# A one-core three-block network: norm roots, pair sums and final squares put in another order

## The reference, cut to what matters

```python
def rms_norm(x, g):                     # before every part
    return x * rsqrt(mean(x * x, -1) + 1e-6) * g
def sq_relu_mlp(h, w_up, w_down):       # 1024 -> 4096 -> 1024, twice
    return square(relu(h @ w_up)) @ w_down
# layer 0: x += rglru_mixer(norm(x)); x += sq_relu_mlp(norm(x), ...)
# layer 1: x += dsa_mixer(norm(x));   x += sq_relu_mlp(norm(x), ...)
# x = rms_norm(x, final_norm_g)
# second network: h = rmsnorm(x); q, k, v, r, lr, u, g_a, g_b = split(h @ w_in)
#   linear attention over chunks of 64 with decays from lr; gates; x += merged @ w_out
#   gate, up = split(rmsnorm(x) @ w_ffn_in); x += (silu(gate) * up) @ w_ffn_out   # 2816 wide
# out = rmsnorm(x, norm_final)
```

## Time and profile before

| | us |
|---|---|
| median of 3 runs (lowest to highest) | 1854.32 (1854.08 to 1855.75) |
| profiled execution | 1855.39 |
| its span, first to last instruction | 1854.1 |
| TensorE busy | 1809.6 |
| VectorE, ScalarE, GpSimd busy | 1301.1, 797.7, 282.8 |
| mean granted TensorE clock | 0.989 |

### The profile page before, as it was taken

The page is one execution under the profiler, slowest core; times in us unless marked ns, Lnnn a source line. Parts: engine busy times, 40 slices in busy tenths (PEclk is TensorE's granted clock), DMA queues, the critical chain, the costliest instruction groups (busy, mean ns, idle before and its releaser), DMA issues.

```text
span 1854.1 us, 21884 instructions
## 1 busy us (share of the span) xinstructions
PE 1809.6 (98%) x8584; PEld 1463.9 (79%) x8584; DVE 1301.1 (70%) x1694; ACT 797.7 (43%) x1046; POOL 282.8 (15%) x227
## 2 busy tenths in 40 slices
PE   9999899999999999899999989999999999999998
PEld 7788688888877668688888868788787888788886
DVE  7885878686879865677786857766446446856757
ACT  6743434343444863334343344555323333323324
POOL 0004000000145864000000051111001321001010
PEclk9999899999999999999999989999999999999999
DMA  6233150522233103341405022221332324331411
GB/s 229 91 114 113 46 161 30 173 91 91 64 97 121 40 4 111 113 140 43 159 25 180 21 80 81 79 68 60 95 97 89 104 69 159 100 127 47 148 57 57
DMA packets 146374, 174.98 MB, mean 94 GB/s; under 512 B 7296, under 2 KB 120064, under 8 KB 146272
## 3 DMA queue, kind: packets, MB, share of 16 engines
q1 hardware_dynamic: 144256, 166.45, 27.6%
q0 software_dynamic: 2016, 7.14, 1.1%
HBM read 171.31 MB, written 2.14 MB: 94 GB/s over the span
## 4 chain that ended last, share of the span: by engine, by line
PE 85%; DVE 5%; issue 4%; ACT 3%; POOL 2%; DMA 0%; SPq 0%; DVEq 0%; POOLq 0%; ACTq 0%
PE bank L968 26%; PE bank L970 26%; PE bank L969 26%; PE bank L1004 1%; PE bank L1183 1%; DVE wlo L1995 1%; PE bank L1209 1%; ACT whi L1447 1%; DVE XC L2092 1%; PE bank L1320 1%; PE bank L1338 1%; POOL Hw L952 1%; DVE rstd L2011 1%; PE bank L1187 1%; POOL wlo L772 0%
## 5 line engine op out<-in xcount | busy, mean ns | idle before, releaser
L968 PE MATMUL bank<-Ahi,whi 128*128 128x512 f32 x1400 | 552.0, 394 | 12.4 <-DVE wlo L1995 5.8
L970 PE MATMUL bank<-Ahi,wlo 128*128 128x512 f32 x1400 | 546.1, 390 | 0.0
L969 PE MATMUL bank<-Alo,whi 128*128 128x512 f32 x1400 | 546.0, 390 | 0.0
L1995 DVE TENSOR_TENSOR wlo<-stage,whi 128x2048 fp32r<-128x2048 f32 (+1 forms) x133 | 306.4, 2304 | 158.6 <-ACT whi L1447 158.5
L1447 ACT ACTIVATE whi<-stage 128x2048 fp32r<-128x2048 f32 (+1 forms) x139 | 262.6, 1889 | 228.5 <-PE bank L970 203.1
L968 PEld LDWEIGHTS bank<-Ahi,whi 128*128 128x128 f32 x1400 | 262.9, 188 | 78.2 <-DVE wlo L1995 8.0
L970 PEld LDWEIGHTS bank<-Ahi,wlo 128*128 128x128 f32 x1400 | 262.8, 188 | 56.3
L969 PEld LDWEIGHTS bank<-Alo,whi 128*128 128x128 f32 x1400 | 263.0, 188 | 55.3 <-issue 1.2
L968 PE MATMUL bank<-whi,Hh 128*128 128x512 f32 x602 | 238.2, 396 | 15.9 <-issue 13.8
L969 PE MATMUL bank<-wlo,Hh 128*128 128x512 f32 x602 | 236.5, 393 | 0.0
L970 PE MATMUL bank<-whi,Hl 128*128 128x512 f32 x602 | 236.4, 393 | 0.0
(11 more groups left out here) (358 smaller groups left out, 2467.3 us busy)
## 6 DMA issues: line engine op xcount, KB each, us to landing
stage<-in_mlp_w_up SPq DMA_DIRECT2D x32, 1024.0 KB, 5.4
stage<-in_w_in SPq DMA_DIRECT2D x22, 1024.0 KB, 5.1
stage<-in_w_ffn_in SPq DMA_DIRECT2D x22, 1024.0 KB, 4.9
quad<-in_mlp_w_down SPq DMA_DIRECT2D x16, 1024.0 KB, 6.1
stage<-in_mlp_w_down SPq DMA_DIRECT2D x16, 1024.0 KB, 4.9
stage<-in_rec_w_in SPq DMA_DIRECT2D x6, 1024.0 KB, 5.3
stage<-in_att_w_in SPq DMA_DIRECT2D x6, 1024.0 KB, 5.3
stage<-in_rec_w_out SPq DMA_DIRECT2D x4, 1024.0 KB, 5.7
```

The source lines that it names most:

```text
L968: e.matmul(ps, hi, rh, start=first, stop=False, skip_group_check=onto)
L969: e.matmul(ps, hi, rl, start=False, stop=False, skip_group_check=onto)
L970: return e.matmul(ps, lo, rh, start=False, stop=last, skip_group_check=onto)
L1995: e.tensor_tensor(lo_of(u)[:, 0:nk, 0:n], source(u), f32(hi_of(u)[:, 0:nk, 0:n]), ALU.subtract).then_inc(s_lo[slot_of[u]], 1)
```

## The change

- MLP and feed-forward part: the root matmul stands after block 0, not after block 1.
- MLP, on VectorE and ScalarE: `first_of_pair` of a pair stands behind the relu of its second tile, `second_of_pair` behind the relu of the next tile, `low_sums` a pair later; `high_sums` behind the next square; weights' low halves ahead of the relu.
- The differences: in group 0 (`early(key)` false) T3 is formed inside the slab, after the sums of product 1, and after T2; T1 is formed a step later. In other groups T1 and T3 stay ahead of the slab. In the feed-forward part `first_of_pair` stands ahead of the difference.
- The high half of the second unit after an MLP (qi0, Q0) is made inside the last slab.
- Linear attention: ScalarE makes all eight Ahi and then the sixteen squares, then K0's and V0's high halves; VectorE makes the low halves of Q0, K0 and V0 one behind the other. The two norm matmuls stand after qk1 and use banks 6 and 7 outside the ring.
- The end: partial squares of half rows in a tile of their own (ysum), the gain multiplied in by GpSimd, rows 0 and 1 and the right halves of rows 2 and 3 scaled by ScalarE.

```diff
-            if m == 1:
+            if m == 0:
...
     pair(("Q", 0), ("qk", 2))
-    ring.add("ss", "ss2")
     pair(("K", 0), ("qk", 1), ("qk", 3))
...
+    DIFF = [{"T1": 1, "T2": 2, "T3": 3, "T4": 4}, {"T1": 1, "T3": 2, "T2": 3, "T4": 4}]
+
+    LAST = [(0, 0), (1, 0), (0, 1), (1, 1), (2, 1), (3, 1), (2, 0), (3, 0)][:6]
+
+    def early(key):
+
+        return key[-1] > 0
...
+        e.wait_ge(s_cols, 32)
+        for i, (j, h) in enumerate(LAST):
+            e.wait_ge(s_ysq, i + 1)
+            e.tensor_tensor(sum_of(j, h), sum_of(j, h), fin2b[:, h * 512:h * 512 + 512], ALU.mult).then_inc(s_yw, 1)
...
         product(("qk", 2), s, 128, Ahi, Alo)
-        ps = begin("ss")
-        e.wait_ge(s_tsp, 14)
-        e.matmul(ps[:, :], ones[:, :], sqa_e[:, :], start=True, stop=True).then_inc(*ring.put("ss"))
-        ps = begin("ss2")
-        e.matmul(ps[:, :], ones[:, :], sqb_e[:, :], start=True, stop=True).then_inc(*ring.put("ss2"))
         s = take_unit(("K", 0))
         product(("qk", 1), s, 0, Ahi, Alo)
+        e.wait_ge(s_tsp, 14)
+        e.matmul(banks[6][:, :], ones[:, :], sqa_e[:, :], start=True, stop=True).then_inc(s_ss, 1)
+        e.matmul(banks[7][:, :], ones[:, :], sqb_e[:, :], start=True, stop=True).then_inc(s_ss, 1)
         product(("qk", 3), s, 128, Ahi, Alo)
...
                     turn_x(1, 0, 1)
+                    root("root_f", "ffn")
                 product(("fg", g, j + 1), s, 128, Ahi, Alo)
                 if g == 0 and j == 0:
                     turn_x(1, 2, 3)
-                    root("root_f", "ffn")
...
                         squared(l, 8 * g + 2 * mm - 1)
                     for u in w[mm]:
                         hi(u)
+                    if mm == 0 and g == 0:
+                        std_of(("root", l), 1024)
+                    squared(l, 8 * g + 2 * mm)
                     if mm:
                         high_sums(n0 + mm - 1)
-                    elif g == 0:
-                        std_of(("root", l), 1024)
-                    squared(l, 8 * g + 2 * mm)
                 squared(l, 8 * g + 7)
                 after = u_of[(*key, "T4")] + 1
-                slab_hi(key, [after, after + 1] if g < 3 else [after])
+                slab_hi(key, [after, after + 1])
...
             scaled_hi(m, gfm[:, m:m + 1])
-            if n == 7:
-                hi(u_of["lr"] + 1)
-            for i, (acc, t, kw) in enumerate(((sqa_e, sqt_e, {}), (sqb_e, sqs_e, {"scale": c1("fin1", m)}))):
-                if n > 2:
-                    e.wait_ge(s_tsp, 2 * (n - 3) + i + 1)
-                e.activation((t[n % 2] if n else acc)[:, :], X[:, m, :], ACT.Square, **kw).then_inc(s_tsa, 1)
+            if n < 7:
+                return
+            for n, m in enumerate(TURN):
+                for i, (acc, t, kw) in enumerate(((sqa_e, sqt_e, {}), (sqb_e, sqs_e, {"scale": c1("fin1", m)}))):
+                    if n > 2:
+                        e.wait_ge(s_tsp, 2 * (n - 3) + i + 1)
+                    e.activation((t[n % 2] if n else acc)[:, :], X[:, m, :], ACT.Square, **kw).then_inc(s_tsa, 1)
...
-        hi(u_of["Q", 0] + 1)
-        e.wait_ge(*ring.full("ss"))
-        e.activation(std[:, :], ring.bank("ss")[:, :], ACT.Sqrt, bias=epsc[:, 0:1], scale=1.0 / 1024).then_inc(s_std, 1)
-        e.wait_ge(*ring.free("ss2"))
+        hi(u_of["K", 0])
+        hi(u_of["V", 0])
+        e.wait_ge(s_ss, 1)
+        e.activation(std[:, :], banks[6][:, :], ACT.Sqrt, bias=epsc[:, 0:1], scale=1.0 / 1024).then_inc(s_std, 1)
+        e.wait_ge(s_ssr, 2)
         e.activation(sqt2[:, :], sqb_e[:, :], ACT.Sqrt).then_inc(s_std, 1)
-        hi(u_of["K", 0] + 1)
-        hi(u_of["K", 0] + 2)
+        hi(u_of["V", 1])
...
+        last_square(0, 0, 0, 1)
+        last_square(1, 1, 0, 1)
+        last_square(2, 0, 1, 4)
+        last_square(3, 1, 1, 4)
+        e.wait_ge(s_ysq, 4)
         for j in range(2):
-            e.wait_ge(*product_read(key, 4, j))
-            e.wait_ge(*product_read(key, 1, j))
-            if j:
-                e.wait_ge(s_ysq, j)
-            e.activation(junk[:, :], D[j][:, :], ACT.Square, accum_out=oss[:, j:j + 1]).then_inc(s_ysq, 1)
-        e.wait_ge(s_ysq, 2)
-        e.activation(rtok[:, 0:2], oss[:, 0:2], ACT.Sqrt, bias=epsc[:, 0:1], scale=1.0 / 1024).then_inc(s_yroot, 1)
+            last_root(j)
+        last_square(4, 2, 1, 5)
+        last_square(5, 3, 1, 5)
         for j in range(2):
-            e.wait_ge(*product_read(key, 5, j))
-            e.wait_ge(s_ysq, 2 + j)
-            e.activation(junk[:, 0:512], sum_of(2 + j, 1), ACT.Square, accum_out=oss[:, 4 + j:5 + j]).then_inc(s_ysq, 1)
-        for j in range(2):
-            e.wait_ge(*product_read(key, 6, j))
-            e.wait_ge(s_ysq, 4 + j)
-            e.activation(junk[:, 0:512], sum_of(2 + j, 0), ACT.Square, accum_out=oss[:, 2 + j:3 + j]).then_inc(s_ysq, 1)
+            last_scale(j, 0).then_inc(*st.inc())
+            last_scale(j, 1).then_inc(s_yg, 1)
...
+                if r == 1 and not early(key):
+                    difference(key, "T3")
                 if r == 2:
                     difference(key, "T4")
...
                         relu(l, 8 * g + 2 * mm - 1)
-                        if mm > 1:
-                            for u in w[mm][:-1]:
-                                lo(u)
+                        first_of_pair(q0 + mm - 1, (s_q, n0 + 2 * mm - 1))
+                    if mm > 1:
+                        low_sums(q0 + mm - 2)
+                    for u in w[mm]:
+                        lo(u)
+                    if mm == 0 and g == 0:
+                        root(("root", l), f"mlp{l}")
+                    if mm == 3 - early(key):
+                        difference(key, "T1")
+                    if mm == 3 and early(key):
+                        difference(key, "T3")
+                    relu(l, 8 * g + 2 * mm)
+                    if mm:
                         second_of_pair(q0 + mm - 1, (s_q, n0 + 2 * mm))
-                        lo(w[mm][-1])
-                        if mm > 1:
-                            difference(key, ("T1", "T3")[mm - 2])
-                        low_sums(q0 + mm - 1)
-                    else:
-                        lo(w[0][0])
-                        if g == 0:
-                            root(("root", l), f"mlp{l}")
-                    relu(l, 8 * g + 2 * mm)
-                    first_of_pair(q0 + mm, (s_q, n0 + 2 * mm + 1))
+                first_of_pair(q0 + 3, (s_q, n0 + 7))
+                low_sums(q0 + 2)
...
-        lo(u_of["lr"] + 1)
-        lo(u_of["Q", 0] + 1)
+        lo(u_of["Q", 0])
+        lo(u_of["K", 0])
+        lo(u_of["V", 0])
...
-                if j == n - 2:
+                if j == n - 2 and early(key):
...
+                first_of_pair(q, (s_fu, fcount[g, j] + 1))
                 if j == n - 2:
-                    difference(key, "T3")
-                first_of_pair(q, (s_fu, fcount[g, j] + 1))
+                    difference(key, "T3" if early(key) else "T1")
...
+                part(0, 0, 0)
+                part(1, 0, 1)
+                over(0)
+                over(1)
+                part(2, 1, 4)
+                part(3, 1, 5)
+                e.wait_ge(s_cols, 32)
+                add_sum(key, 6, 0, False)
+                add_sum(key, 6, 1, False)
+                for j in (2, 3):
+                    over(j)
+                    e.wait_ge(s_yrec, 5 + j)
+                    e.scalar_tensor_tensor(sum_of(j, 0), sum_of(j, 0), gnh[:, j:j + 1], fin2b[:, 0:512], ALU.mult, ALU.mult).then_inc(s_yt, 1)
```

More of the change, by code:

```diff
@@ L463, in ring_ffn @@
         for j in range(0, FG[g][1], 2):
-            pair(("fg", g, j), ("fg", g, j), ("fg", g, j + 1))
+            ring.add(("fg", g, j))
             if g == 0 and j == 0:
                 ring.add("root_f")
+            pair(("fg", g, j), ("fg", g, j + 1))
             pair(("fu", g, j), ("fu", g, j), ("fu", g, j + 1))
@@ L997, in gemm @@
                 product((*name, m), s, m % 2 * 128, hi, lo, nk=nk, ready=ready if m == first else None, n0=n0)
-                if m == 1 and hook:
+                if m == 0 and hook:
                     hook()
@@ L1439, in hi @@
                 else:
-                    e.wait_ge(s_diff, 4 * slab_no[key] + {"T1": 1, "T3": 2, "T2": 3, "T4": 4}[name])
+                    e.wait_ge(s_diff, 4 * slab_no[key] + DIFF[early(key)][name])
             else:
@@ L1949, in scalar_program @@
                 if g == 0 and j == 0:
-                    for x in range(4, 8):
-                        keep_x(x)
+                    keep_x(4)
+                    keep_x(5)
                     std_of("root_f", 1024)
+                    keep_x(6)
+                    keep_x(7)
                 gate_root(g, j)
@@ new lines, in last_root, with last_scale @@
+        def last_root(j):
+            e.wait_ge(s_yrec, (1, 2, 5, 6)[j])
```

(21 more changed lines are left out.)

65 lines of the change are left out of this document (29 added, 36 removed).

## The result

The kernel after takes **1834.22 us** (median of 4 runs, 1833.20 to 1834.98); the kernel before, on the same chip, 1854.20. The ratio is 0.989, with a 95% interval of 0.9873 to 0.9907. The forecast was 1829, with 1826 to 1833 as its own range and 1820 to 1838 with the rivals; the result lies 1.2 above the narrower one. The profiled execution took 1834.98 against 1855.39 before: 20.4 us less, where my sum had 25.05.

A forecast was written before the change was run, and what follows sets the result against it. TensorE, busy 98% of the span, was the bound; only holes and half clock could go. 21.7 + 2.55 + 1.3 - 0.5 = 25.05 off 1855.39 gave 1830.3, or 1829 as median; range 1826 to 1833, with rivals 1820 to 1838.

The forecast's parts named there:

- The up blocks: Both MLPs, group 0: earlier root, lagged pair sums and T3's move close the 6.7 us holes and their half clock; 21.7 us.
- (a): MLP up blocks: the root matmul one block earlier brings the reciprocal 4.8 us earlier, at up to 0.35 us of new wait.
- T3 inside the slab: Group 0 slabs: T3 just fits in the MLPs, 0 us; feed-forward loses 1.2 in the slab, gains 2.55 net.
- rival 2: Group 0 slabs: T3 makes products 3 to 5 wait, with half clock behind, 11 us in all; 1840; 13%.
- Linear attention: Squares last shorten early waits but open a 6.4 us hole at K0, with half clock behind; net gain 1.3 us.
- The rule that I weighed: Linear attention: two-input VectorE and SBUF-reading GpSimd instructions exclude each other, first one keeps the port; sum 0.35 worse.
- The end: Kernel's end: VectorE has less before the last sums, ScalarE takes four scalings; -0.5 us, bounds -1.5 to +1.5.
- Rival 4: All eight MLP slabs: the lag makes relu 7 late, about 4.5 us a slab, 36 in all; slower, 1865; 4%.
- Rival 3: MLP up blocks: relu 6 stays late behind B21's high half, so some 5 of the 21.7 us remain; 1846; 8%.
- Rival 1: Linear attention: the squares do not hold K0's high half up; 1821; 12%.

The follow-up runs named there:

- Experiment 10: The kernel after, with the pair sums and low sums of both MLPs back in the order of the kernel before; 1837.99 us.
- Experiment 2: The kernel after, with the first sum of product 5 ahead of the next part's low half in the three slabs of group 0; 1829.13 us.
- experiment 3: The kernel after, with T1 and T3 both formed ahead of the slab in group 0 too; 1834.24 us.
- experiment 9: The kernel after, with both MLPs' root back behind up block 1 and T1 and T3 ahead of the slab in group 0; 1838.78 us.
- Experiment 1: The kernel after, with K0's high half on ScalarE behind the sixth of the 16 squares instead of the sixteenth; 1828.29 us.
- experiment 4: The kernel after, with the linear attention's squares spread again between the operands' high halves, two behind each; 1831.83 us.
- experiment 6: The kernel after, with only the root of both MLPs back behind up block 1; 1838.87 us.
- experiment 7: The kernel after, with K0's high half behind the sixth square and product 5's first sum ahead of the next low half in group 0; 1825.54 us.
- experiment 8: The kernel of experiment 7, with twelve of the 14 adds of squares moved from GpSimd to VectorE behind K0's low half; 1819.59 us.

## Why the prediction was right, and where it was off

**The up blocks: right in mechanism, 21.1 forecast for the MLPs, 19.9 measured.** The reciprocal came where (a) put it, and the relus to within 0.6 us. Two terms were missing from the sum, of opposite sign, so that 19.9 is so near to 21.1 is in part luck. Product 6's wait took 2 x 1.25; without it the MLPs would have given 22.4. And the groups 1 to 3, to which I gave nothing, brought 1.6: 202.4 us in each MLP against 203.0 and 203.3 before. Experiment 10, without the lag, has 203.0 and 203.3 again, so this is the lag's. The root, which (a) put at 4.8 us an MLP, by itself gave 4.6 in the second and 5.4 in the first. What I did not see is that the lag alone would have given most of it.

**T3 inside the slab: the step that failed in the MLPs.** I followed VectorE up to the sum that frees the bank of product 4, found that "in the MLPs this just fits", and took 0, with 1 as the bound. The chain was right up to there: no product before the last waits. I stopped two products early: the low half that the slab owes to the next group comes before the sum of product 5. In the feed-forward slab the wait at product 3 did not come, that at product 4 was 0.7 (0.8 forecast), and that at product 6 cost another 1.26; the waits together are 0.8 more than forecast, about half of the way from 3.2 to 1.7; the rest I have not found. Experiment 2 gave 1.35 back in each of the three. With T3 ahead of the slab (experiments 3 and 9) product 6 does not wait. It is rival 2's mechanism one product further on and at a third of its price: 3.8 us of its 11, and no half clock behind.

**Linear attention: the hole was foreseen, its size was not; +1.3 became -0.95.** Term by term: the loss at the transposes 0.94 (0.9 forecast); at Q0's low half 1.4 (1.9); GpSimd's adds 1.25 apart (1.22); the last square ended as summed. The hole is 8.4 and not 6.4. Of these 2.0, 1.3 are K0's low half, 4.48 where I took half of 6.38, that is 3.2. The stretch at half clock behind it cost 1.7 (2.2 forecast), and a second one of 3.40 us, 1.7 more, was in no step; the 0.9 forecast for the small transposes and the gate did not come. These terms make 1.8 of the 2.25. Experiment 1 shows that the hole hung on one line's place in ScalarE's queue, and experiment 4 that the squares' place by itself moves the time by 0.4. Where the norm matmuls stand, and the order of the three low halves, was not tested alone. The rule that I weighed, of the Trainium skill (SBUF — State Buffer, Who interferes with whom), was right where rows now bear on it: Q0's low half, first at the port, kept its 2.29 (1062.85 to 1065.14), and the first add took 2.47. Its sum, 0.35 worse than mine, lay on the right side; at "at most one add" my reading of it failed, since K0's low half stood behind two.

**The end: -0.2, where I had -0.5.** Not tested by itself.

**Rival 4** (relu 7 late in all eight slabs) did not occur: relu 7's bank is waited for in no slab of the kernel after, and by 0.9 us only when the root or T3 stands in the way. **Rival 3** neither: relu 6 came early. Rival 1 (K0 not held up, 1821) did not occur either; experiment 1 builds it, and it gives 7.5 us of the section where the rival had 8.6.

## What to carry to other kernels

When an instruction is moved into a chain that only just fits, follow the chain to the end of the stage, with every instruction that the stage does for the next one: what breaks is the first bank behind the point where you stop adding up. Before work is put ahead of an operand in a queue, ask whether that work waits for another engine; the operand inherits the wait (16 squares were 10.7 us of ScalarE's work and took 16.3). And where a slower engine carries a chain of small adds (1.26 us each) and a faster one (0.68) sits idle beside it, look at moving the adds: here it was worth 4.8 us of the section.

## What the runs showed of the hardware

**A waiting low half can stand behind two adds.** K0's low half alone takes 2.29 us. Beside GpSimd's adds of the same tiles it took 4.48 in the kernel after: the adds of 1079.93 and 1081.16 both ran in their usual 1.26, and the low half ended 2.15 us after the second. In experiment 3 it met the adds in the same way and ran behind one only, the next add paying:

```profile
1080.87 3.32 POOL L911 TENSOR_TENSOR sq_e<-sq_e,sq_e 128x512 f32<-128x512 f32 x1
```

In experiment 1 the record of K0's low half starts 0.18 before that of an add: 2.37, and the add 3.33. In all these pairs one of the two stood still while the other ran at its full speed. Which of them it is moved 1.3 to 2 us of TensorE's time between kernels that differ elsewhere. What decides it no run shows, and it is not the distance of the starts: a low half that started 0.15 to 0.18 us after an add stood behind two adds in the kernel after and in experiments 1 (V0's), 2, 6 and 10, but behind one in experiment 7 (V0's, 0.16), and behind one at 0.19 in experiments 3 and 9.

**Half clock did not follow every hole.** Behind the holes of 6.9 to 8.4 us the clock was always at 0.50, for 2.8 to 5.9 us from the hole's end on the earlier trace rows. Behind holes of about 2 it was there in some places and not in others: in experiment 9 the same hole of 2.0 was followed by none in the first MLP and by 3.4 us in the second. The stretch at 1101.7, behind the small matmuls of the gate, came without a hole over 0.3 us, in the kernel after and in experiments 3, 4, 6, 8, 9 and 10, and not in 2. In 8 there is no large hole and no half clock ahead of it, so it is not an echo of K0's. A forecast of a small hole should carry 0 to 1.7 us for it.
